# The routed outputs of an MoE layer: rows of 28 pairs of experts gathered and added within the last four iterations, the outputs of the last four pairs combined on TensorE

## The reference

```python
# x = rmsnorm(h); gate[n, e] is not zero for 8 of 64 experts of each row n
h_e    = silu(x @ w_gate[e]) * (x @ w_up[e])        # 1024 -> 256, for each expert e
routed = sum over e of gate[n, e] * (h_e @ w_down[e])   # 256 -> 1024
shared = (silu(x @ ws_gate) * (x @ ws_up)) @ ws_down
y = rmsnorm(h + routed + shared) * normf_g
```

## Time and profile before

| | us |
|---|---|
| median of 3 runs | 1245.03 |
| profiled execution, whole | 1237.07 |
| its span, first to last instruction | 1235.3 |
| the expert part begins (first add of input and mix) | 572.4 |
| last matmul ends | 1176.3 |
| TensorE busy in the span | 964.6 (78%) |
| VectorE busy | 500.5 (41%) |
| GpSimd busy | 323.4 (26%) |

### The profile page before, as it was taken

The page is one execution under the profiler, slowest core; times in us unless marked ns, Lnnn a source line. Parts: engine busy times, 40 slices in busy tenths (PEclk is TensorE's granted clock), DMA queues, the critical chain, the costliest instruction groups (busy, mean ns, idle before and its releaser), DMA issues.

```text
span 1235.3 us, 17206 instructions
## 1 busy us (share of the span) xinstructions
PE 964.6 (78%) x7091; PEld 569.7 (46%) x7091; DVE 500.5 (41%) x921; ACT 211.1 (17%) x444; POOL 323.4 (26%) x378
## 2 busy tenths in 40 slices
PE   4897998899889976397888887778887888887800
PEld 4676676767776764233643333333233333332200
DVE  2148749847874988533424111111011111110037
ACT  3231123114101411203001111111111111111101
POOL 0029606921880494000011011110011101110052
PEclk9998999899999987788789988999889988889865
DMA  7341443054225204771229999999999999999644
GB/s 241 106 136 45 171 144 108 11 206 148 78 98 171 87 11 158 283 313 29 101 89 373 410 411 404 378 391 400 399 404 402 397 406 385 400 397 395 255 168 171
DMA packets 97049, 298.92 MB, mean 242 GB/s; under 512 B 17030, under 2 KB 48168, under 8 KB 80311
## 3 DMA queue, kind: packets, MB, share of 16 engines
q1 hardware_dynamic: 80471, 254.02, 54.3%
q0 software_dynamic: 16496, 43.74, 9.6%
HBM read 275.47 MB, written 39.45 MB: 255 GB/s over the span
## 4 chain that ended last, share of the span: by engine, by line
PE 42%; DMA 28%; DVE 19%; SPq 4%; issue 3%; ACT 2%; POOL 1%; POOLq 0%; DVEq 0%; ACTq 0%
PE bank L1049 40%; DMA big<-in_w_up 23%; DMA big<-in_w_in 3%; SPq L361 3%; DVE big L1582 2%; DVE big L875 2%; ACT big L1323 1%; DVE big L1700 1%; DVE big L1558 1%; DMA big<-in_g_up 1%; DVE big L1552 1%; POOL big L936 1%; DVE big L1617 1%; DVE big L1549 1%; DVE big L1623 1%
## 5 line engine op out<-in xcount | busy, mean ns | idle before, releaser
L1049 PE MATMUL bank<-big 64*64 64x64 f32 (+5 forms) x6666 | 908.0, 371 | 187.2 <-DMA big<-in_w_up 91.5
L1049 PEld LDWEIGHTS bank<-big 64*64 64x64 f32 (+3 forms) x6666 | 521.3, 157 | 525.9 <-issue 390.9
L1323 ACT ACTIVATE big<-bank 128x512 f32<-128x512 f32 (+10 forms) x287 | 122.7, 450 | 763.1 <-PE bank L1049 455.7
L792 DVE TENSOR_TENSOR big<-big,bank 128x256 f32<-128x256 f32 x32 | 13.5, 421 | 359.1 <-ACT big L1323 359.1
L906 POOL DMA_INDIRECT yrows<-big x32 | 32.4, 1012 | 450.4 <-PE bank L506 367.5
L1754 POOL TENSOR_SCALAR big<-big 128x256 f32<-128x256 f32 x120 | 128.3, 1070 | 0.4
L1766 POOL TENSOR_TENSOR big<-big 128x256 f32<-128x256 f32 x120 | 83.5, 696 | 0.3
L1582 DVE SCALAR_TENSOR_TENSOR big<-big 128x256 f32<-128x256 f32 x120 | 71.7, 598 | 3.8
L1750 POOL TENSOR_SCALAR big<-big 128x256 f32<-128x256 f32 x4 | 2.4, 594 | 201.7 <-DVE big L1542 201.7
L884 POOL DMA_INDIRECT big<-xg,big x32 | 32.4, 1012 | 84.5 <-DVE big L773 54.4
L1323 ACT ACTIVATE big<-big 128x16 f32<-128x16 f32 (+5 forms) x70 | 30.5, 486 | 125.6 <-DVE big L699 48.8
(11 more groups left out here) (148 smaller groups left out, 424.0 us busy)
## 6 DMA issues: line engine op xcount, KB each, us to landing
big<-in_w_gate SPq DMA_DIRECT2D x64, 1024.0 KB, 15.2
big<-in_w_up SPq DMA_DIRECT2D x64, 1024.0 KB, 17.6
big<-in_w_down SPq DMA_DIRECT2D x64, 1024.0 KB, 10.1
big<-in_w_in SPq DMA_DIRECT2D x29, 1024.0 KB, 5.5
yrows<-big POOLq DMA_DIRECT2D x32, 512.0 KB, 6.5
big<-in_w_out SPq DMA_DIRECT2D x2, 2048.0 KB, 10.6
big<-in_x_prompt SPq DMA_DIRECT2D x2, 1024.0 KB, 7.3
big<-in_state_wkv SPq DMA_DIRECT2D x32, 64.0 KB, 2.2
```

Source lines behind the costliest of these rows:

```text
L1049: return nc.tensor.matmul(out_, lhsT=lhsT, rhs=rhs, start=start, stop=stop)
L1323: return nc.scalar.activation(out_, in_, f, **kw)
```

## The change

Pairs 28 to 31 are "late" (NLATE = 4, FIRST = 28).

- Their results are not scattered. For each late pair VectorE makes a matrix of gates by token and slot (`late_gates`: one-hot times gate), TensorE transposes it (`turn_gates`), VectorE copies it into `GT`. TensorE then multiplies GT by `ye` (`combine`), six matmuls of 512 columns for three tiles of tokens and two halves, and VectorE adds each from PSUM to xrow (`add_late`). combine(28) and (29) stand at the start of iterations 30 and 31, combine(30) behind the last gate_up, combine(31) at the end. They go through three PSUM banks, the last one through six.
- The gates of pairs 28 and 29 are made at the start of iteration 29, those of 30 and 31 at the start of iteration 30, on TensorE and on VectorE.
- When the scatter of pair 27 has landed, GpSimd starts the 24 gathers, into six buffers `early`; rows of late pairs are out of bounds and skipped, and their gate is set to zero. From gather 6 on it waits for an add to free the buffer. VectorE adds gathers 0 to 7 at the end of its pair(29), 8 to 15 at the end of pair(30), 16 to 23 in pair(31) ahead of take(30).
- In iteration 31 down(30) is moved between the two halves of gate_up(31), and store(30) on ScalarE ahead of the sigmoid.
- The count is read at pair 4 instead of at the end, on four engines. Five small operations after pair 0 prepare masked gates and row numbers. GpSimd clears four of the new buffers before its first fetch.
- Outputs are written tile by tile.

The diff, cut; left out are the branches for over 64 tokens per expert, semaphore names, and two renamed semaphores in VectorE's part.

```diff
--- before
+++ after
...
+        GT = [x[:, j, :] for x in (hsh, sgs) for j in range(2)]
...
+        OHg = bibm.rearrange("p (t x n) -> p t x n", t=3, x=2)
...
+        gate8e, gate8l, rowl = E.take(3, 8), E.take(3, 8), E.take(3, 8).bitcast(U32)
...
+        NLATE = 4
+        FIRST = NPAIR - NLATE
+        NEB = 6
...
+        early = [x2p[:, i, :] for i in range(3)] + [E.take(D) for _ in range(NEB - 3)]
...
-            return 16 * len(range(b, NPAIR, NYE))
+            return 16 * len(range(b, FIRST, NYE))
...
+        TAIL = (0, 2, 1)
...
+        COMB = tuple((t, h) for t in TAIL for h in range(2))
+        ROW_LIMIT = 2 * SLOTS * FIRST
+
+        def comb_bank(q, n):
+            return ps[(1, 2, 0, 3, 5, 6)[n]] if q == NPAIR - 1 else ps[(1, 2, 0)[n % 3]]
...
-            sp.wait_ge(S['fin_ready'], 3)
-            sp.dma_start(out['y_p'][0].rearrange("(t p) d -> p t d", p=128), xrow[:, 0:2, :]).then_inc(S['fin_out'], 16)
-            sp.dma_start(out['y_s'][:, 0, :], xrow[0:NS, 2, :]).then_inc(S['fin_out'], 16)
-            sp.wait_ge(S['fin_out'], 32)
...
+            for n, t in enumerate(TAIL):
+                sp.wait_ge(S['fin_ready'], n + 1)
+                dst = out['y_p'][0, 128 * t:128 * t + 128, :] if t < 2 else out['y_s'][:, 0, :]
+                sp.dma_start(dst, xrow[0:tile_rows(t), t, :]).then_inc(S['fin_out'], 16)
+            sp.wait_ge(S['fin_out'], 48)
...
             def turn(q):
 
                 pe.wait_ge(S[f'gath{q % NXE}'], 16 * (q // NXE + 1))
+                if q == NPAIR - 1:
+                    pe.wait_ge(S['cb_sum'], 6)
...
+            def turn_gates(q):
+
+                pe.wait_ge(S['og_ready'], q - FIRST + 1)
+                pe.wait_ge(S['idx_ready'], 2 * NPAIR)
+                wait(pe, 'g_ready', q - FIRST)
+                for t in range(3):
+                    r = tile_rows(t)
+                    ins = nc.tensor.transpose(ps_idx[:, 128 * t:128 * t + r],
+                                              OHg[0:r, t, :, :].rearrange("p x n -> p (x n)"), ident[0:r, 0:r])
+                note(ins, 'g_mm')
+
+            def combine(q):
+
+                pe.wait_ge(S['g_ready'], NLATE)
+                pe.wait_ge(S['ye_act'], q + 1)
+                pe.wait_ge(S['ye_dve'], q + 1)
+                pe.wait_ge(S['xet_ready'], 2 * min(q + 3, NPAIR))
+                for n, (t, h) in enumerate(COMB):
+                    r = tile_rows(t)
+                    i = 6 * (q - FIRST) + n
+                    wait(pe, 'cb_sum', 6 * (q - FIRST) if q == NPAIR - 1 else i - 2)
+                    note(mm(comb_bank(q, n)[0:r, :], GT[q - FIRST][:, 128 * t:128 * t + r],
+                            ye[q % NYE][:, 512 * h:512 * h + 512]), 'cb_mm')
+
             for q in range(NPAIR):
                 if q + 3 < NPAIR:
                     index(q + 3)
+                if q in (FIRST + 1, FIRST + 2):
+                    turn_gates(2 * q - FIRST - 2)
+                    turn_gates(2 * q - FIRST - 1)
+                if q >= FIRST + 2:
+                    combine(q - 2)
+                if q == 4:
+                    count = pe.value_load(cnti[0:1, 0:1])
                 gate_up(q, 0, 4)
                 if q:
                     turn_hidden(q - 1)
+                if q == NPAIR - 1:
+                    down(q - 1)
                 gate_up(q, 4, KT)
-                if q:
+                if 0 < q < NPAIR - 1:
                     down(q - 1)
                 if q + 1 < NPAIR:
                     turn(q + 1)
+            combine(NPAIR - 2)
             turn_hidden(NPAIR - 1)
             down(NPAIR - 1)
...
+                    pe.wait_ge(S['ov_act'], 3 * NE * c)
+                    pe.wait_ge(S['ov_dve'], 5 * NE * c)
+            combine(NPAIR - 1)
...
             def store(q):
 
                 act.wait_ge(S['yx_mm'], q + 1)
-                wait(act, f'y_out{q % NYE}', 16 * (q // NYE))
+                if q < FIRST + NYE:
+                    wait(act, f'y_out{q % NYE}', 16 * (q // NYE))
+                else:
+                    act.wait_ge(S['cb_mm'], 6 * (q - NYE - FIRST + 1))
...
             for q in range(NPAIR):
                 if q:
                     hidden_turned(q - 1)
+                if q == NPAIR - 1:
+                    store(q - 1)
                 sigma(q)
-                if q:
+                if q == 4:
+                    act.wait_ge(S['cnt_ready'], 1)
+                    count = act.value_load(cnti[0:1, 0:1])
+                if 0 < q < NPAIR - 1:
                     store(q - 1)
                 if q + 1 < NPAIR:
                     turned(q + 1)
...
             def take(q):
                 dve.wait_ge(S['yx_mm'], q + 1)
-                wait(dve, f'y_out{q % NYE}', 16 * (q // NYE))
+                if q < FIRST + NYE:
+                    wait(dve, f'y_out{q % NYE}', 16 * (q // NYE))
+                else:
+                    dve.wait_ge(S['cb_mm'], 6 * (q - NYE - FIRST + 1))
                 note(v.tensor_copy(ye[q % NYE][:, 512:1024], ps_y[1][:, :]), 'ye_dve')
...
+                if q in (FIRST + 1, FIRST + 2):
+                    late_gates(2 * q - FIRST - 2)
+                    late_gates(2 * q - FIRST - 1)
+                if q >= FIRST + 2:
+                    add_late(q - 2)
+                if q == NPAIR - 1:
+                    add_early(16, 24)
+                    take(q - 1)
                 hidden(q)
-                if q:
+                if 0 < q < NPAIR - 1:
                     take(q - 1)
+                if q in (FIRST + 1, FIRST + 2):
+                    add_early(8 * (q - FIRST - 1), 8 * (q - FIRST))
+
+            def late_gates(q):
+                wait(dve, 'g_mm', q - FIRST)
+                link(v.tensor_tensor(OHg, K['slot'][:, 0:SLOTS].unsqueeze(1).unsqueeze(1)
+                                     .broadcast_to([128, 3, 2, SLOTS]),
+                                     posm[:, :, 2 * q:2 * q + 2].unsqueeze(3).broadcast_to([128, 3, 2, SLOTS]),
+                                     ALU.is_equal), chain)
+                note(v.tensor_tensor(OHg, OHg, gate[:, :, 2 * q:2 * q + 2].unsqueeze(3)
+                                     .broadcast_to([128, 3, 2, SLOTS]), M), 'og_ready')
+                dve.wait_ge(S['g_mm'], q - FIRST + 1)
+                note(v.tensor_copy(GT[q - FIRST], ps_idx[:, 0:NT]), 'g_ready')
+
+            def add_late(q):
+                dve.wait_ge(S['early_sum'], 8 * min(q - FIRST + 1, 3))
+                for n, (t, h) in enumerate(COMB):
+                    r = tile_rows(t)
+                    i = 6 * (q - FIRST) + n
+                    dve.wait_ge(S['cb_mm'], i + 1)
+                    wait(dve, 'cb_sum', i - 5)
+                    x = xrow[0:r, t, 512 * h:512 * h + 512]
+                    note(v.tensor_tensor(x, x, comb_bank(q, n)[0:r, :], AD), 'cb_sum')
+                    if q == NPAIR - 1 and h == 1:
+                        dve.wait_ge(S['cb_sum'], i + 1)
+                        note(v.memset(den[:, 0:1], 0.0), 'sum_ready')
+
+            def add_early(k0, k1):
+                wait(dve, 'cb_sum', 6 * (k0 // 8))
+                for k in range(k0, k1):
+                    t, j = TAIL[k // 8], k % 8
+                    r = tile_rows(t)
+                    dve.wait_ge(S[f'early_in{k % NEB}'], 16 * (k // NEB + 1))
+                    wait(dve, 'early_sum', k)
+                    note(v.scalar_tensor_tensor(out=xrow[0:r, t, :], in0=early[k % NEB][0:r, :],
+                                                scalar=gate8e[0:r, t, j:j + 1], in1=xrow[0:r, t, :], op0=M, op1=AD),
+                         'early_sum')
...
             link(v.tensor_scalar(rowf, code8, -1.0, None, AD), chain)
+            link(v.scalar_tensor_tensor(out=gate8e, in0=rowf, scalar=float(ROW_LIMIT), in1=gate8, op0=ALU.is_lt, op1=M),
+                 chain)
+            link(v.scalar_tensor_tensor(out=gate8l, in0=rowf, scalar=float(PASS), in1=gate8, op0=ALU.is_ge, op1=M), chain)
+            link(v.tensor_scalar(code8, rowf, float(PASS), float(4 * MAXPASS * PASS), ALU.is_lt, M), chain)
+            link(v.tensor_tensor(code8, code8, rowf, AD), chain)
+            link(v.tensor_copy(rowl, code8), chain)
             link(v.tensor_copy(rowu, rowf), 'code_ready')
             for q in range(1, NPAIR):
                 pair(q)
+                if q == 4:
+                    count = dve.value_load(cnti[0:1, 0:1])
+            add_late(NPAIR - 2)
             take(NPAIR - 1)
-            count = dve.value_load(cnti[0:1, 0:1])
...
+            add_late(NPAIR - 1)
             dve.wait_ge(S['grow_in'], 32)
...
-            for n, t in enumerate(TAIL):
-                r = tile_rows(t)
-                for j in range(8):
-                    if j == 0 or (j == 4 and t < 2):
-                        dve.wait_ge(S[f'back_in{q}'], 64 if t < 2 else 128)
-                        q += 1
-                    link(v.scalar_tensor_tensor(out=xrow[0:r, t, :], in0=back[0:r, t, j, :], scalar=gate8[0:r, t, j:j + 1],
```

(59 more changed lines are left out.)

21 lines of the change are left out of this document (10 added, 11 removed).

## The result

The changed kernel takes 1253.26 us (median of 7 runs, 1249.70 to 1258.46), the kernel before 1245.03 (median of 7, 1236.08 to 1247.32). The ratio is 1.0078, with a 95% interval of 1.0044 to 1.0113: slower, by 8 us (0.8%).

The account below looks back on a forecast made before the run. Weights bound the expert loop, then a serial 59.0 us tail. The last early add at 1167.4 plus 77.0 us gave a span of 1244.4, 9 us over 1235.3; with the 1245.0 us median, 1254 us, range 1235 to 1260.

Parts of the forecast that it names:

- both stalls: TensorE waiting at the top of iteration 30 for late gates, and within combine(29) in iteration 31, some 8 us.
- S: End of VectorE's last add of gathers 0 to 7 in iteration 29, put at 1167.4 us.
- Gathers beside loads: Early gathers during weight loads: gather 0 lands at 1138.7 us, the next seven 3.9 us apart.
- Rival 1: Iteration 29: gathers not held back by loads, adds back to back to 1149.5 us; 1236 us in all, chance 0.25.
- Gates, combine(28), stall of iteration 31: Iterations 30 and 31: gates 4.8 us, combine(28) 7.4; eight-row adds of 10.5 us then hold up combine(29).
- combine(30): TensorE behind gate_up(31): 5.2 us, with no wait expected for VectorE.
- Just level: Iteration 31: VectorE's adds and copy end at S + 52.0, gate_up(31) on TensorE at S + 52.1.
- The missing term: Between last down and combine(31): only the evacuation, 0.75 us, was counted, then 5.2 us for combine(31).
- Finishes and store: End of the tail: VectorE's three finishes of 1.48 us each, then 3.6 us for the store.
- Gathers during adds: Gathers issued while VectorE adds: a slip of 1 to 3 us in all was weighed and left out.

Follow-up runs that it names:

- the other order: Changed kernel with gates of pairs 30 and 31 made earlier, combine(28) moved to iteration 31 and early adds regrouped around TensorE's needs; 1224.75 us, ratio 0.9830.

## Why the prediction was right, and where its sum was wrong

The sign, the mechanism and the place of both stalls were right. That 1254.0 us came within 1 us of 1253.3 is luck: in the stretch the sum gave 123.7 (46.7 to S, 77.0 behind it) where 126.0 were measured (41.8 and 84.2). Two errors of 4.9 and 7.2 us partly cancel, and the rest is covered by before's short stretch: between these two kernels the stretches differ by 3.2 us more than the medians.

- **Gathers beside loads.** Issue and first landing were right: gather 0 lands 17.8 us after pair 27's evacuation, predicted 18.0. The spacing of 3.9 us was the term that failed: 3.2 on average. One load for one gather held for two landings (3.7 and 3.8, as in the earlier trace rows). The Trainium skill, "DMA: Bandwidth & Descriptors", "Queues, rings and completion order", has each DMA engine go round its queues, a packet at a time. It does not speak of whole transfers: one load for each gather was the prediction's reading of it, which agrees with these two landings and not with the next four, where two gathers, 2.5 to 2.8 us apart, landed per load. There was "a load to alternate with nearly to the end", as the prediction had it: the next burst was issued at 1150.1, before the last load of the old one landed at 1155.4, and the DMA engines were full (a share of 1.0) from 1139.5 to 1171 us. What failed is one for one. Why two gathers then pass per load no run shows.
- **Rival 1, adds back to back, 0.25.** The run without the late loads shows what it would have given: adds back to back, S at 31.5 us (the rival had 28.8, 1149.5 less 1120.7) and 83.8 behind it (77.0), a stretch of 115.2, no shorter than before's, and a median only 1.5 us lower. 2.2 of the 2.7 us by which its S is late are pair 28's evacuation, 20.5 us after pair 27's where the prediction took 18.3. The chance of 0.25 for a faster kernel hung on a tail that was priced too low.
- **Gates, combine(28), stall of iteration 31.** Gates 5.0 (predicted 4.8), combine(28) 8.5 (7.4), to pair 29's evacuation 11.8 (11.8), eight-row adds 11.0 (10.5), the rest of combine(29) 5.8 (5.6). For combine(28) the clock cost more than was taken: the granted clock was 0.50 in 1177 to 1181 us (1.2 GHz throughout) and 0.79 to 1185.5, after 22 us of idling and the few transposes of the gates.
- **combine(30).** 6.9 us for 5.2: VectorE's adds and copy of pair 30 ended at 1226.9, 1.2 us after gate_up(31). "Just level" has no margin.
- **The missing term.** From the end of the last down to combine(31) the sum had 0.75 us; 3.56 were measured, and the combine behind it took 7.34 for 5.2 with the clock down. Together 4.9 us, two thirds of the tail's error. The diff shows that combine(31) stands behind the four branches; the trace of before could not price them, since TensorE has no work behind them there. A bound from both sides was due and not given.
- **Finishes and store.** 5.0 and 3.1 us for 5.4 and 3.6.
- **Gathers during adds.** Gathers issued while the eight-row adds ran (1199.32 to 1209.41) are 1.44 us apart, without adds beside them (1140.87 to 1146.06) 1.30. There is a slip, 0.14 us each, and at most 0.3 us of it is on the path (gather 14 takes 1.30 us on GpSimd in place of 0.99). In the run without early gathers it is larger, with gathers 1.51 us apart on average and single ones up to 2.1, and there the adds wait for them. The rule in the Trainium skill, "SBUF — State Buffer", "Who interferes with whom", that was weighed for it has the right sign in these runs; a slip of an add (1.3 us) each is not seen in any.

Not seen in the prediction: what the run without early gathers showed, that the combining alone costs 18 us ahead of the tail, more than the whole loss. The sum had the pieces (4.8 for gates, 5.2 for a combine), but inside a stall, never set against the 3 us of slack per pair.

## What to carry to other kernels

Work that is moved beside a loop bound by weights is hidden only if every engine's own order lets it: before moving it, write down what is queued behind the first instruction that waits for a slow transfer, and put what another engine needs ahead of it. When two causes may cover one stall (adds, and the landing of a gather that those adds release), take both away before judging either. Price every instruction between the last two steps of the chain, branches that are not taken included.

## What the runs showed of the hardware

- Four branches that are not taken cost TensorE 2.6 us more than one (3.56 and 0.95 us of gap), 4.3 in the other order (5.63 and 1.29), and behind these gaps the granted clock of the next twelve matmul records was 0.77 and 0.68, and they took 7.34 and 8.22 us in place of 5.70. The gap alone does not decide it: in the run without early gathers the same twelve followed a gap of 3.23 us and took 5.69 us at a clock of 1.00. There combine(30) followed gate_up(31) without a pause, where TensorE stood still for 1.43 us in the kernel after and 0.98 in the other order; whether that is the reason was not tried. The Trainium skill, "Advanced Engine Details and Errata", "Control Flow Timing", has some 108 ns for a compare-and-branch, which would make an estimate of 0.3 us for the three that were saved; the runs show eight times that and more, and they decide. What in the branches takes so long (the compare, the jump over the long bodies, the code behind them) wasn't tried.
- An indirect gather of 128 rows that lands 4.4 to 6.7 us after its issue when alone took 8.4 to 17.3 us beside weight loads (where up to five others were queued ahead of it), and they landed 2.5 to 4.5 us apart.
